# Second layer's conditioning: vector multiply-and-add in the first layer's merge in place of matmuls in gated unit and route

## What is computed

```python
mod = jax.nn.silu(c) @ w_ada[i] + b_ada[i]
sh1, sc1, gt1, sh2, sc2, gt2 = jnp.split(mod[:, None, :], N_MOD, axis=-1)
modc = jax.nn.silu(c_ctx) @ w_ada[i] + b_ada[i]
...
h = modulate(rmsnorm(x, g_norm1[i]), sh1, sc1)
...
x = x + gt1 * branch_merge(ya, yb, yc, gates, w_branch[i], w_out[i])
h2 = modulate(rmsnorm(x, g_norm2[i]), sh2, sc2)
x = x + gt2 * ec_moe(h2, w_router[i], w_e1[i], w_e3[i], w_e2[i])
```

## Time and profile before

| | us |
|---|---|
| median of 3 runs (2784.83 to 2790.24) | 2788.16 |
| profiled execution | 2788.38 |
| its span | 2786.4 |
| mean granted TensorE clock, share of full | 0.98 |

### The profile page before, as it was taken

The page is one execution under the profiler, slowest core; times in us unless marked ns, Lnnn a source line. Parts: engine busy times, 40 slices in busy tenths (PEclk is TensorE's granted clock), DMA queues, the critical chain, the costliest instruction groups (busy, mean ns, idle before and its releaser), DMA issues.

```text
span 2786.4 us, 36544 instructions
## 1 busy us (share of the span) xinstructions
PE 2534.9 (91%) x15220; PEld 1805.0 (65%) x15220; DVE 1044.3 (37%) x1528; ACT 880.5 (32%) x1392; POOL 424.2 (15%) x222
## 2 busy tenths in 40 slices
PE   7999989999999999899999888888999998987787
PEld 7888878899998777688863222224777895322223
DVE  4548532326764444544441011113474653000001
ACT  4465544344444344422331100002344442000001
POOL 1430016771001232100220000000133011000000
PEclk9999999999999999899999999999999999999999
DMA  5434327764544221323269999999213448999997
GB/s 211 157 137 153 119 77 280 299 240 174 185 156 152 76 72 46 151 91 121 96 265 397 429 428 429 429 429 377 101 61 133 152 151 361 425 429 429 429 430 316
DMA packets 66510, 668.27 MB, mean 240 GB/s; under 512 B 7328, under 2 KB 8496, under 8 KB 10544
## 3 DMA queue, kind: packets, MB, share of 16 engines
q1 hardware_dynamic: 64368, 655.48, 59.2%
q0 software_dynamic: 1984, 10.51, 1.0%
HBM read 664.89 MB, written 1.06 MB: 239 GB/s over the span
## 4 chain that ended last, share of the span: by engine, by line
PE 54%; DMA 22%; DVE 5%; ACT 3%; issue 2%; PEld 2%; POOL 1%; DVEq 0%; POOLq 0%; PEldq 0%; ACTq 0%
PE ps L605 12%; PE ps L607 12%; PE ps L606 12%; DMA ring<-in_blocks 10%; PE ps L2508 9%; DMA hi_place<-in_blocks 7%; DMA WK<-in_blocks 5%; PE ps L825 1%; PE ps L2019 1%; PE ps L794 1%; POOL A L1805 1%; PE ps L633 1%; PE ps L811 1%; PE ps L613 1%; ACT WK L869 1%
## 5 line engine op out<-in xcount | busy, mean ns | idle before, releaser
L605 PE MATMUL ps<-A,piece_hi 128*128 128x256 f32 (+1 forms) x1952 | 617.8, 316 | 19.7 <-ACTq L485 7.2
L606 PE MATMUL ps<-A,piece_hi 128*128 128x256 f32 (+1 forms) x1952 | 605.2, 310 | 0.0
L607 PE MATMUL ps<-A,ring_lo 128*128 128x256 f32 (+1 forms) x1952 | 604.7, 310 | 0.0
L498 ACT ACTIVATE piece_hi<-ring 128x1024 fp32r<-128x1024 f32 x378 | 393.1, 1053 | 202.0 <-DVEq L644 104.8
L509 POOL TENSOR_TENSOR ring_lo<-ring,piece_hi 128x1024 fp32r<-128x1024 f32 x123 | 312.7, 2554 | 680.2 <-ACT piece_hi L498 622.5
L605 PEld LDWEIGHTS ps<-A,piece_hi 128*128 128x128 f32 x1952 | 377.4, 193 | 58.2 <-issue 24.7
L507 DVE TENSOR_TENSOR ring_lo<-ring,piece_hi 128x1024 fp32r<-128x1024 f32 x255 | 316.5, 1246 | 253.7 <-ACT piece_hi L498 253.2
L606 PEld LDWEIGHTS ps<-A,piece_hi 128*128 128x128 f32 x1952 | 377.9, 194 | 17.8
L607 PEld LDWEIGHTS ps<-A,ring_lo 128*128 128x128 f32 x1952 | 377.5, 193 | 18.1
L2659 DVE TENSOR_TENSOR A_place<-A_place,ps 128x512 f32<-128x512 f32 x32 | 22.0, 688 | 539.4 <-PE ps L2508 539.4
L1047 POOL TENSOR_TENSOR WK<-WK 128x512 f32<-128x512 f32 (+1 forms) x36 | 40.5, 1125 | 1025.5 <-ACT WK L1041 1024.8
(11 more groups left out here) (295 smaller groups left out, 3283.6 us busy)
## 6 DMA issues: line engine op xcount, KB each, us to landing
ring<-in_stream SPq DMA_DIRECT2D x237, 1024.0 KB, 4.9
ring<-in_blocks SPq DMA_DIRECT2D x82, 2048.0 KB, 25.1
WK<-in_blocks SPq DMA_DIRECT2D x39, 2048.0 KB, 25.6
extra<-in_blocks SPq DMA_DIRECT2D x28, 2048.0 KB, 25.6
hi_place<-in_blocks SPq DMA_DIRECT2D x28, 2048.0 KB, 25.6
A_place<-in_blocks SPq DMA_DIRECT2D x11, 2048.0 KB, 34.6
WK<-in_na_bias POOLq DMA_DIRECT2D x2, 2048.0 KB, 8.0
WK<-in_blocks SPq DMA_DIRECT2D x4, 1024.0 KB, 28.3
```

Of the source, the lines that this page charges most:

```text
L498: nc.scalar.activation(piece_hi[:, no % 4, :], ring[:, slot, at:at + PIECE], ACT.Copy).then_inc(hi_done[no % 4], 1)
L605: nc.tensor.matmul(out_, l[0], r[0], start=first, stop=False)
L606: nc.tensor.matmul(out_, l[0], r[1], start=False, stop=False)
L607: return nc.tensor.matmul(out_, l[1], r[0], start=False, stop=last)
```

## The change

The second layer's conditioning leaves the stream: its 24 steps on TensorE, with their copies and turns, and 24 transfers of the ring go. In place of them the host lays the matrix out with the outputs in the partitions: 48 groups of 128 outputs, 128 x 1024 words each (`dots`). GpSimd's queue loads them one by one into three places (two in `extra`, one in `WK`), and VectorE makes for each group a `tensor_tensor_reduce`: product with the vector, sum along the row, bias as the start value, result to `MOD`. For the first 16 groups it does so for both vectors, for the other 32 for `c` alone: 64 instructions. They stand in the merge of the first layer: two groups behind the second and two behind the fourth gate piece, one behind each of the four projected banks, eight in a section. The vectors, broadcast to all partitions, come to `extra` by a transfer in the first block, and ScalarE applies Silu to them at the start of `down_act`. Since `extra` is in use until then, SyncE issues all first blocks after the last ring transfer and after the last group (`near` last). Gated unit and route have all eight banks, and the route in layer 0 has eight idle products where it had four.

```diff
-    + LAYERS * ((12 + 8) * TILE + 3 * 2 * (TILE + BC * 512) + 2 * TILE)
+    + 12 * TILE + LAYERS * (8 * TILE + 3 * 2 * (TILE + BC * 512) + 2 * TILE)
...
-ADA_GROUPS = {0: ((0, 0), (0, 1), (0, 2)), 1: ((1, 0), (1, 1), (1, 2))}
-ADA_NO = {group: n for n, group in enumerate(ADA_GROUPS[0] + ADA_GROUPS[1])}
+ADA_GROUPS = {0: ((0, 0), (0, 1), (0, 2))}
+ADA_NO = {group: n for n, group in enumerate(ADA_GROUPS[0])}
...
-        at += MIX_PIECES - MERGE_PIECES
-        if layer == 0:
-            steps(1, range(DC), 0)
-        at += MERGE_PIECES
-        if layer == 0:
-            steps(1, range(DC, 3 * DC), 0)
+        at += MIX_PIECES
...
+        COND = extra[:, 0:2 * D]
+        DOT_WORDS = [extra[:, 2 * D:3 * D], extra[:, 3 * D:4 * D], wk(16640, D)]
+        DOT_OUT = wk(16640 + D, D)
+
+        def dots_pool(pool):
+
+            for i in range(MODC):
+                if i >= 3:
+                    pool.wait_ge(dot_used, i - 2)
+                pool.dma_start(DOT_WORDS[i % 3], a["dots"][i]).then_inc(dot_landed[i % 3], 16)
+
+        def dot_dve(dve, steps, i):
+
+            if i == 0:
+                dve.wait_ge(cond_ready, 1)
+            else:
+                dve.wait_ge(dot_used, i)
+            dve.wait_ge(dot_landed[i % 3], 16 * (i // 3 + 1))
+            at = MODC + i
+
+            def dot(s):
+                return nc.vector.tensor_tensor_reduce(DOT_OUT, DOT_WORDS[i % 3], COND[:, s * D:(s + 1) * D], 1.0, ada_par[:, at:at + 1],
+                                                      ALU.mult, ALU.add, MOD[:, at, s:s + 1])
+            if i < 2 * DC:
+                steps(dot(1))
+            dot(0).then_inc(dot_used, 1)
+
+        def merge_dve(dve, cur, steps, branches, kc, n, y, ada=None, dots=False):
...
+            def next_dots(count):
+                nonlocal dot
+                for _ in range(count if dots else 0):
+                    dot_dve(dve, steps, dot)
+                    dot += 1
...
                         skip_fm(dve, cur, 2)
                         behind_two()
+                        next_dots(2)
 
...
                             return nc.vector.tensor_tensor(m, m, GATE[:, j, 0:n], ALU.add)
                         read_bank(dve, cur, True, op, piece=(kc == DC or j % 2 == 1))
+                        next_dots(1)
                         if (j + 1) * kc % (2 * DC) == 0:
...
 
         def down_act(act, cur):
+            act.wait_ge(cond_load, 16)
+            nc.scalar.activation(COND, COND, ACT.Silu).then_inc(cond_ready, 1)
             split_x_act(act, cur, [(FH[:, s, :], FHR[:, 0, s, :]) for s in FGROUPS])
...
         def gmlp_pe(pe, cur, tt, layer, lam_init):
-            if layer == 0:
-                for slot in range(4):
-                    ada_pe(pe, cur, 1, slot)
-
-            def behind_sums():
-                if layer == 0:
-                    for slot in range(4, DC):
-                        ada_pe(pe, cur, 1, slot)
-            head_norm_pe(pe, cur, da_norm(tt * P, lam_init), between=behind_sums)
+            head_norm_pe(pe, cur, da_norm(tt * P, lam_init))
...
-                if layer == 0:
-                    ada_dve(dve, cur, 1, DC - 1)
...
-            step = {-1: 8, 3: 9, 5: 10}
             b = cur.bank()
             if cur.taken_before():
                 pe.wait_ge(bank_free[b], cur.bank_use())
-            if ada:
-                ada_pe(pe, cur, 1, step[-1])
...
-                if ada and k in step:
-                    ada_pe(pe, cur, 1, step[k])
...
-            if ada:
-                ada_pe(pe, cur, 1, 11)
...
-            if ada:
-                for slot in range(12, 16):
-                    ada_pe(pe, cur, 1, slot)
-            idle_bank(pe, cur, 4 if ada else 8)
+            idle_bank(pe, cur, 8)
             pe.wait_ge(placed, cur.base("route") + 1)
             bank_parts(pe, cur, [(P, m * 64, 64, [(PLACE[0:64, m * P:(m + 1) * P], ident[0:64, 0:64])]) for m in range(2)], turn=True)
-            if ada:
-                for slot in range(16, 18):
-                    ada_pe(pe, cur, 1, slot)
...
-                    at = DC * s + c
-                    if ada and at % 2 == 1 and at < 12:
-                        ada_pe(pe, cur, 1, 18 + at // 2)
             cur.add("h2", tt)
-            if ada:
-                ada_pe(pe, cur, 1, 24)
...
-            if ada:
-                ada_dve(dve, cur, 1, 15)
...
-            if ada:
-                ada_dve(dve, cur, 1, 16)
...
-            if ada:
-                ada_dve(dve, cur, 1, 23)
-                ada_dve(dve, cur, 1, 24)
...
-            run(R, EXPERTS_AT[0] // 2 - 20)
-            load_block(0, 0)
-            run(EXPERTS_AT[0] // 2 - 20, EXPERTS_AT[0] // 2 - 10)
-            first_blocks(0, [1, 2])
-            run(EXPERTS_AT[0] // 2 - 10, EXPERTS_AT[0] // 2)
-            first_blocks(0, [3, 4, 5, 6])
+            run(R, EXPERTS_AT[0] // 2)
+            sp.wait_ge(dot_used, MODC)
+            first_blocks(0, [0, 1, 2, 4, 5, 6, 3])
...
-                merge_dve(dve, cur, steps, 3, BC, n, Y2)
+                merge_dve(dve, cur, steps, 3, BC, n, Y2, dots=layer == 0)
...
-                if layer == 0:
-                    ada_dve(dve, cur, 1, 8)
...
+            nc.gpsimd.memset(MOD[:, :, :], 0.0).then_inc(cs_zero, 1)
...
+            pool.dma_start(COND, a["cond"].partition_broadcast(P)).then_inc(cond_load, 16)
...
                 lows(pool, cur)
+                if layer == 0:
+                    dots_pool(pool)
                 mix_lo_pool(pool, cur, n, range(DC))
...
+        "dots": x["w_ada_2"][1].T.reshape(MODC, P, D), "cond": np.concatenate([x["c_2"][0], x["c_ctx_2"]]),
```

More of the change, by code:

```diff
@@ L439, in build @@
         cs_zero = sem("cs_zero")
+        cond_load = sem("cond_load")
+        cond_ready = sem("cond_ready")
+        dot_landed = [sem(f"dot_landed{i}") for i in range(3)]
+        dot_used = sem("dot_used")
         cs_ready = sem("cs_ready")
@@ L2427, in route_pool, with route_dve @@
             cur.add("route", 1)
-        def route_dve(dve, cur, steps, st, ada):
+        def route_dve(dve, cur, steps, st):
             tt = 2 * st
@@ L2921, in _ @@
                     barrier(pe, cur)
-                cur.set_ring(range(6) if layer == 0 else range(NB))
+                cur.set_ring(range(NB))
                 gmlp_pe(pe, cur, n // P, layer, 0.0)
@@ L3288, in _stream @@
             f(w, at * BW, (at + 1) * BW)
-        if l == 0:
-            for slot in range(DC):
-                ada(1, slot)
         for n in range(3):
@@ L3298, in _stream @@
         fm(x["w_out_2"][l], 0, D)
-        if l == 0:
-            for slot in range(DC, 3 * DC):
-                ada(1, slot)
         for e in range(EXPERTS):
```

13 lines of the change are left out of this document (6 added, 7 removed).

## The result

The median of the kernel after is 2805.38 us (2803.78 to 2806.83, 4 runs) against 2789.11 for the kernel before in the same runs: ratio 1.0057, 95% interval 1.0044 to 1.007, so it is slower. The profiled executions have spans of 2803.6 and 2786.4 us, 17.2 apart. The medians are 16.3 apart. The forecast was +9.3, and its range reached +22.6.

A forecast was written before the change was run, and what follows sets the result against it. TensorE, busy 91%, was taken as the bound, with time following the experts' first matmul. Merge 17.8 + down 1.9 + gated unit 0.8 - route 11.2 = +9.3 us, so 2797.5 us; range 2784.5 to 2811.

The forecast's parts named there:

- What sets the time: Start of first expert stage: the kernel's time moves as the experts' first matmul, at 1480.43, moves.
- Rival B: First expert stage bound by transfers from its first block; removed ring bytes save 24.4 us: 2784.5 us; chance 0.07.
- Route: Layer 0's route without conditioning steps: four pieces gain 11.2 us together, between 9.7 and 12.7.
- First stretch: Start of route: logits come earlier, then ScalarE itself is late next; gain 1.6 us.
- tail: Route, from the gather's end to the experts' first matmul: 2.8 us shrinks to layer 1's 0.8, gain 2.0.
- Merge, sections 0 and 1: First merge sections: VectorE becomes the bound and TensorE waits for its splits, 10.9 us with three small instructions.
- Merge, the end: End of merge: GpSimd's low parts start late behind the dot products' transfers, costing 6.9 us.
- only just covered: End of merge: VectorE's remaining work ends about when GpSimd reaches its eighth low part; without cover, 1 or 2 us more.
- Down: Down stage: the Silu ahead of ScalarE's splits of the hidden rows costs 1.9 us.
- Gated unit: Gated unit: one copy of 0.68 us saved, 1.5 us possibly lost to TensorE's lower clock; +0.8 taken.
- Rival A: Merge: VectorE's slack suffices and only the tail counts, -1.6 us: 2786.8 us; chance 0.18.
- Rival C: Merge: each dot product runs at half rate, 2.3 us, lengthening the merge by about 51 us: 2831 us; chance 0.13.

The follow-up runs named there:

- even_fill: Kernel after with all dot products in merge sections 0 to 4, mostly behind gate-piece splits, Silu moved, ten idle products in the gated unit: 2782.40 us, ratio 0.9974.
- no_dots: Kernel after without the 64 dot products and their 48 transfers: 2786.87 us, ratio 0.9993.
- spread: Kernel after with the 16 groups of two dot products spread over the first 40 groups, last section unchanged: 2797.71 us, ratio 1.0023.
- pool_gap: Kernel after with a waited-for one-column clear ahead of each of GpSimd's low-part subtractions: 2807.93 us, ratio 1.0058.
- last_free: Kernel after with no dot products in the merge's last section and more in sections 2 to 4: 2794.99 us, ratio 1.0018.
- after_again: Kernel after, unchanged, run and traced a second time: 2802.65 us, ratio 1.0054.
- one_source: Kernel after with the last section's eight dot products replaced by plain sums with one SBUF input: 2799.21 us, ratio 1.0051.
- double: Kernel after with every dot product made twice, same transfers: 2863.44 us, ratio 1.027.

## Why the prediction was right, and where it was not

The sign was right, and the time lies in the range; the size was 8 us short of the 17.2 measured in the spans. The 16.3 of the medians are beyond the sum's own upper bound of +15.8. Only the widening of the range to 2811, made for an instruction dearer than thought, takes the result in, and the instruction was cheaper: that part was luck. Against the terms:

- **What sets the time** (the experts' first matmul): right. It moved from 1480.43 to 1494.99, +14.6, and the expert stage then lasted 0.4 longer, although 10.5 MB had gone from the transfers ahead of it. Rival B is out.
- **Route**, -11.2 forecast, -11.9 and -11.8 measured. First stretch 1.7 (forecast 1.6; from the stage's mark to the places 24.4 before, 22.7 now); from places to gather 5.9 before, 1476.77 - 1473.81 = 3.0 now, so 2.9 (2.7); gather 17.39 (17.5), gain 5.0 (4.9); tail 1494.99 - 1494.16 = 0.8, gain 2.0 (2.0). Layer 1 as a model of layer 0 without conditioning was good to 0.2 us, the cold start of the gather included. Between variants the stage differs by up to 3.6 us (-8.5 to -12.1), more than my bounds of 9.7 to 12.7.
- **Merge, sections 0 and 1**: 10.9 forecast. The mechanism and its places were right, the size too large: the three waits are 1.7, 1.8 and 2.3 where I had 3.1, 4.2 and 3.0, and TensorE's last gate bank came 7.1 later (5.3 in the second trace). The term that was mis-sized is the time from one start to the next: I had 2.8 for a group of two and 1.23 for a split, and the rows show 2.5 (1220.11 to 1222.64) and 1.13. By these rows, as an estimate, VectorE has some 32.5 us of work in section 0 instead of 35.4, and 34.8 in section 1 instead of 37.7, where the sections last 32.7. So in section 0 TensorE waits because the work is crowded behind the banks, not because its sum is too large.
- **Merge, the end**: 6.9 forecast for GpSimd's late start. It starts 204.0 us after the merge's first product instead of 190.4, +13.6; less the 7.1, 6.5. Right. The step that failed is the next one, "only just covered". GpSimd's eight took 16.6 instead of 14.3 (+2.3), since VectorE's operations with two SBUF inputs in that stretch do not run beside them but in turn; and TensorE, waiting 6 us there in small pieces, made its output products at the lower clock (0.69 from 1392 to 1414; 1.00 from 1371 to 1393 in before): the 18.6 less 13.6 and 2.3, 2.7. Together 5.0 where I had 0, and up to 2 in the bound. The two errors, -3.8 and +5.0, nearly cancel in 18.6 against 17.8: the merge's total was right by luck in part.
- **Down**, +1.9 forecast, +2.9 measured. The wait grew from 0.82 to 2.62, 1.8, as forecast; 1.1 more came behind it (granted clock 0.97 in that stretch, 1.00 before). Moving the Silu takes away both.
- **Gated unit**, +0.8 forecast, +2.1 measured. I took the clock's price from the gather of rows 7, 1.5; here the idle time ahead of the sums went from 1.29 to 5.94 us and they took 6.96 instead of 4.72. The term of the clock, 1.5, is 2.2 by these rows (granted clock 0.50 during the sums), and even_fill takes it back. The 0.7 that the copy was to give does not show: the sums start 1.7 us ahead of the mark at 1157 in both kernels, and the stage grows by nearly all of the 2.2.
- **Not forecast**: +2.7 before the down stage and +1.7 in layer 1, and 0.9 behind the last mark (which the second trace of before has too, 0.8). Up to 671 us no instruction was added but a clear and the broadcast of `cond`; ten traces of the changed code and its variants have between -0.3 and +4.5 there, 2.2 on average, the two of before 0.0 and -0.1. Part goes with the clock: from 380 to 396 us it is 0.79 in after and 0.89 in before, and 1.2 of the 2.7 us arise there. Two traces of before are too few to say whether a cost of some 2 us stands behind the scatter. In layer 1 the stretch from 1943 to 2157 is 1.5 to 2.2 longer in all ten, no_dots among them, and not in the second trace of before; its cause stays open. What spread (+3.1) and pool_gap (+5.8) have on top lies behind 2157.
- **Rival A** (slack suffices) is wrong for after, yet nearly true once the 64 are evenly laid and none is in the last section: VectorE is then busy for 23 to 29 of 33 us in each of the first five sections, and TensorE waits 1.1 us in all. **Rival C** is refuted by the 1.28 us. The Trainium skill ("Vector Engine (DVE) Microarchitecture Reference", "Points that are easy to get wrong") has the shape S2S2D2_STT at half throughput with two SBUF sources that are not bf16. The f32 form without a sum is not at half rate here, nor is the dot product; whether the dot product's row, CUSTOM_DVE_ANT_0, is of that shape no run shows.

## What to carry to other kernels

A vector engine at 40% on average has no free 85 us: count own work plus added work in each section, put the added part where the engine has only a split to do, and keep it out of the last section, where a chain of small steps ends the stage. If the added part is put closer together, look again whether its data comes in time: VectorE waits for its transfers in last_free and even_fill where it did not in after. Where two engines both work with two SBUF inputs, do not count their times as parallel; their sum is the safe side (18.3 us here for 16.6 measured). A wait that comes new to TensorE, or an emptier stretch of it, is charged once as a wait and can be charged again as a lower clock behind it (1.1 us in down, 2.2 in the gated unit, 2.7 at the merge's end, nothing behind the splits in the second trace of after); in the gated unit ten idle products took that back.

## What was new about the hardware

- Beside GpSimd's two-input subtractions, VectorE's operations with two SBUF inputs wait: 1.28 to 2.28 us for a dot product, 1.21 to 2.3 for a split, 0.69 to 7.00 for an addition that met five subtractions in a row. With one input from PSUM (0.67 to 0.69) or one SBUF input alone (1.21) there is nothing. The Trainium skill ("SBUF — State Buffer", "Who interferes with whom") says that a VectorE instruction with two SBUF inputs contends with a GpSimd instruction that reads SBUF, and that one with at most one SBUF input, outside the two-port modes, does not; the trace agrees.
- Of the two-port modes the same section of the Trainium skill says that whoever issues first gets the shared ports for the whole instruction. For the two-input addition here the trace shows otherwise: by its row it starts 0.21 us ahead of GpSimd's first subtraction and ends behind the fifth, in all five traces with that timing (after, after_again, spread, one_source, double: 6.94 to 7.03 us).
- A GpSimd subtraction takes 1.25 us when VectorE is shut out, and 1.3 to 2.3 when the two take turns, as in before and last_free, where GpSimd has no gap either. Why VectorE gets its turns there and loses five in after is not shown; with a clear between the subtractions (pool_gap) it gets them.
- Ten idle products of TensorE in a wait of 5.9 us were enough for its next work to run at the full clock (1.00 for 0.50).
